# Level products of keys moved to VectorE, one copy moved earlier on ScalarE, and diagonal scores from summed keys

## The reference

```python
z = h @ w_in                     # q, v, zf, zb, og, u, gz
k = (1.0 - lb) * sigmoid(-z)     # keys kf (forward), kb (backward)
f = exp(log_f)                   # decays, one per channel and token
# per direction, 8 heads of 128 channels:
scores = einsum('t d, t s d, s d -> t s', q, decay, k)   # decay: product of f between s and t
o = scores @ v + (q * exp(b)) @ s_start
o = o_forward + flip(o_backward)
o = o * rsqrt(mean(o * o) + EPS) * hgrn_norm_g * silu(og)
# then the convolution branch, gates, w_out, the router and
# out = sum over the top 8 of 64 experts of silu(h @ gate) * (h @ up) @ down
```

## Time and profile before

| | |
|---|---|
| median of 3 runs | 904.22 us (902.78 to 906.89) |
| the profiled execution | 905.2 us, of which the profiled span is 903.4 us |
| TensorE busy | 831.0 us, 92% of the span |
| VectorE busy | 387.5 us, 43% |
| ScalarE busy | 215.3 us, 24% |
| POOL busy | 91.6 us, 10% |
| moved by DMA | 284.70 MB, mean 315 GB/s |

### The profile page before, as it was taken

One profiled execution on the slowest core, in us unless ns is written; L12 is line 12 of the kernel. 1 busy time (PEld: TensorE's weight loads), 2 busy tenths in 40 slices (PEclk: granted clock), 3 DMA queues, 4 the chain that ended last, 5 costly groups with the idle time before them and its releaser, 6 DMA issues.

```text
span 903.4 us, 12822 instructions
## 1 busy us (share of the span) xinstructions
PE 831.0 (92%) x5242; PEld 561.4 (62%) x5242; DVE 387.5 (43%) x760; ACT 215.3 (24%) x335; POOL 91.6 (10%) x63
## 2 busy tenths in 40 slices
PE   4699999999899999998999999779999999899973
PEld 2388989569899988995535544435554755345221
DVE  1225898369799846736232322111212111112104
ACT  3124443133354334403111111101111101011001
POOL 1000536205243310000000000000000000000000
PEclk9899999999899999979999999979999999999987
DMA  8979878135234538973999999999999999999993
GB/s 316 386 253 338 309 268 317 39 103 174 67 123 135 193 110 268 410 301 119 377 378 418 418 416 415 418 416 417 416 417 410 418 414 417 417 417 417 418 400 142
DMA packets 81173, 284.70 MB, mean 315 GB/s; under 512 B 5208, under 2 KB 11736, under 8 KB 64728
## 3 DMA queue, kind: packets, MB, share of 16 engines
q1 hardware_dynamic: 80760, 283.11, 80.5%
q10 hardware_dynamic: 352, 0.74, 0.3%
HBM read 280.67 MB, written 3.16 MB: 314 GB/s over the span
## 4 chain that ended last, share of the span: by engine, by line
PE 71%; SPq 12%; DMA 10%; DVE 4%; issue 2%; ACT 0%; POOL 0%; DVEq 0%; POOLq 0%
PE bank L1979 14%; SPq L591 10%; PE bank L2028 8%; PE bank L1588 5%; DMA chunk<-in_w_expert_down 5%; PE bank L1590 5%; PE bank L1596 5%; PE bank L1870 4%; PE bank L1893 4%; PE bank L1576 3%; PE bank L1650 3%; PE bank L1630 3%; DMA ring<-in_w_ada 2%; DMA chunk<-in_w_expert_gate_up 2%; PE bank L1544 2%
## 5 line engine op out<-in xcount | busy, mean ns | idle before, releaser
L1979 PE MATMUL bank<-chunk,xg 128*64 128x512 f32 (+2 forms) x1024 | 200.3, 616 | 21.2 <-DMA chunk<-in_w_expert_gate_up 19.9
L1979 PEld LDWEIGHTS bank<-chunk,xg 128*64 128x64 f32 (+2 forms) x1024 | 62.7, 130 | 153.5 <-issue 137.5
L2028 PE MATMUL bank<-chunk,act_t 128*64 128x512 f32 (+2 forms) x512 | 102.3, 623 | 5.1 <-DMA chunk<-in_w_expert_down 5.0
L1407 DVE SCALAR_TENSOR_TENSOR act_r<-bank,w_slot,sil 128x256 f32<-128x256 f32 x26 | 12.5, 482 | 181.5 <-ACT sil L933 181.5
L645 POOL TENSOR_TENSOR small<-small 128x4 f32<-128x4 f32 (+2 forms) x9 | 10.2, 1138 | 599.2 <-DVE small L1484 501.1
L1419 DVE TENSOR_TENSOR y_lo<-bank,y_hi 128x512 fp32r<-128x512 f32 x52 | 36.0, 691 | 76.4 <-ACT y_hi L946 76.4
L2028 PEld LDWEIGHTS bank<-chunk,act_t 128*64 128x64 f32 (+2 forms) x512 | 31.3, 130 | 54.7 <-issue 53.8
L933 ACT ACTIVATE sil<-bank 128x256 f32<-128x256 f32 x26 | 10.0, 385 | 203.4 <-PE bank L1979 203.4
L1032 DVE TENSOR_TENSOR ring_lo<-ring,ring_hi 128x1024 fp32r<-128x1024 f32 x40 | 47.9, 1220 | 20.4 <-ACT ring_hi L742 20.4
L946 ACT ACTIVATE y_hi<-bank 128x512 fp32r<-128x512 f32 x52 | 31.1, 597 | 105.2 <-PE bank L2028 105.2
L1870 PE MATMUL bank<-sel_p,h_hi 128*128 128x256 f32 x208 | 52.4, 293 | 2.3 <-DVE h_lo L1299 2.3
(11 more groups left out here) (293 smaller groups left out, 1323.2 us busy)
## 6 DMA issues: line engine op xcount, KB each, us to landing
chunk<-in_w_expert_gate_up SPq DMA_DIRECT2D x128, 1024.0 KB, 20.6
chunk<-in_w_expert_down SPq DMA_DIRECT2D x64, 1024.0 KB, 22.6
ring<-in_w_in SPq DMA_DIRECT2D x16, 2048.0 KB, 10.6
ring<-in_w_ada SPq DMA_DIRECT2D x12, 2048.0 KB, 13.4
ring<-in_w_proj_hgrn SPq DMA_DIRECT2D x2, 2048.0 KB, 8.1
ring<-in_w_out SPq DMA_DIRECT2D x2, 2048.0 KB, 13.5
ring<-in_w_proj_conv SPq DMA_DIRECT2D x1, 2048.0 KB, 7.8
chunk<-in_w_shared_gate_up SPq DMA_DIRECT2D x2, 1024.0 KB, 23.4
```

The costliest lines, as they stand in the source:

```text
L1979: ins = mm(bank[2 + b][row:row + width, :], xg[:, k, c:c + width], w[:, k % 4, :], start=(k == 0), stop=(k == KD - 1))
L2028: ins = mm(out[row:row + width, :], act_t[:, c, row:row + width], w[:, c, h * 512:(h + 1) * 512], start=(c == 0), stop=(c == 1))
```

## The change

Four things are changed.

- POOL no longer multiplies keys. VectorE does it, ahead of the query products of the same level, after it has read the level's scores. It waits for `mix_done` before it overwrites the keys; what it signals is `k_done` as before.
- ScalarE's copy of blended keys for level 2 stands ahead of the sigmoid of og1's first half, and no longer behind it. The copies of the other levels keep their place. The copy of level 0 waits for the scores of level −1, since `k_mix` and the new `k_sum` share their memory.
- POOL adds forward and backward keys into `k_sum`, the first four heads after their keys, the last four after theirs. TensorE makes the scores of level −1 with one matmul per head and sequence instead of two.
- POOL's inverse root for the convolution's normalisation (L645) was between its products of levels 2 and 3. It now stands alone.

```diff
--- before.py
+++ after.py
@@ -183,6 +183,7 @@
         rows_dw = at("rows_dw", 198, [P, P])
         s_new = at("s_new", 197, [P, 16, P])
         k_mix = at("k_mix", 197, [P, 16 * P])
+        k_sum = at("k_sum", 197, [P, 16 * P])
         w_r = at("w_r", 181, [P, KD, NE])
         c_pad = at("c_pad", 205, [P, KD, 32])
         mod_cols = at("mod_cols", 205, [NS * KD, 2 * P])
@@ -665,22 +666,11 @@
                                                     ALU.mult, ALU.add).then_inc(fk_done, 1)
                             nc.gpsimd.tensor_scalar(qk[:, 2 + d, c], qk[:, 2 + d, c], oml[:, i:i + 1], None,
                                                     ALU.mult).then_inc(fk_done, 1)
-            pool.wait_ge(fk_done, 32)
-
-            for level in range(LEVELS):
-                m = 1 << level
-                if level == 3:
-                    pool.wait_ge(cms_done, 1)
-                    rsqrt(rms_c, ssq_c, 2).then_inc(crms_done, 1)
-                pool.wait_ge(sc_ready, 4 * (level + 2))
-                pool.wait_ge(mix_done, level + 1)
-                if level:
-                    pool.wait_ge(tot_done, level)
-                kf, kb = halves(qk[:, 2, :], level), halves(qk[:, 3, :], level)
-                tf, tb = halves(fg[:, 0, :], level), halves(fg[:, 1, :], level)
-                nb = 16 * P // (2 * m)
-                nc.gpsimd.tensor_tensor(kf[:, :, 0, :], kf[:, :, 0, :], tf[:, :, 1, 0:1].broadcast_to([P, nb, m]), ALU.mult).then_inc(k_done, 1)
-                nc.gpsimd.tensor_tensor(kb[:, :, 1, :], kb[:, :, 1, :], tb[:, :, 0, 0:1].broadcast_to([P, nb, m]), ALU.mult).then_inc(k_done, 1)
+                pool.wait_ge(fk_done, 16 + 17 * half)
+                c = slice(half * 4 * T, (half * 4 + 4) * T)
+                nc.gpsimd.tensor_tensor(k_sum[:, c], qk[:, 2, c], qk[:, 3, c], ALU.add).then_inc(fk_done, 1)
+            pool.wait_ge(cms_done, 1)
+            rsqrt(rms_c, ssq_c, 2).then_inc(crms_done, 1)
             for g in range(4):
                 pool.wait_ge(oms_done, g + 1)
                 rsqrt(rms_o[:, 4 * g:4 * g + 4], ssq_o[:, 4 * g:4 * g + 4], 4).then_inc(orms_done, 1)
@@ -782,7 +772,7 @@
                     act.wait_ge(k_done, 2 * level)
                     act.wait_ge(sc_ready, 4 * (level + 1))
                 else:
-                    act.wait_ge(fk_done, 32)
+                    act.wait_ge(sc_ready, 4)
                 dst = halves(k_mix[:, :], level)
                 nc.scalar.activation(dst[:, :, 0, :], halves(qk[:, 2, :], level)[:, :, 0, :], ACT.Copy)
                 nc.scalar.activation(dst[:, :, 1, :], halves(qk[:, 3, :], level)[:, :, 1, :], ACT.Copy).then_inc(mix_done, 1)
@@ -804,14 +794,16 @@
             for half in range(2):
                 for j in range(2):
                     n = half * 2 + j
+                    if n == 2:
+                        mix_keys(2)
                     filled(act, f"og{half}", j)
                     if n < 2:
                         act.wait_ge(mod_ready, 12)
                     else:
                         evacuated(act, f"og{(n - 2) // 2}", n % 2)
                     nc.scalar.activation(tmp[:, n % 2, :], fill_bank(f"og{half}", j)[:, :], ACT.Sigmoid).then_inc(og_sig, 1)
-                    if j == 0:
-                        mix_keys(1 + half)
+                    if n == 0:
+                        mix_keys(1)
                     split_hi(apart + 1 + half, (3,) if j else (0, 1, 2))
             for name, dst in (("ga", ga), ("gb", gb)):
                 for half in range(2):
@@ -1080,7 +1072,7 @@
 
             score_tiles(-1)
 
-            dve.wait_ge(fk_done, 32)
+            dve.wait_ge(fk_done, 34)
             for d in (1, 0):
                 V.tensor_tensor(qk[:, 1 - d, :], qk[:, 1, :], fg[:, d, :], ALU.mult).then_inc(q_done, 1)
             dve.wait_ge(q_done, 2)
@@ -1122,8 +1114,12 @@
                 nb = 16 * P // (2 * m)
                 qb, qf = halves(qk[:, 0, :], level), halves(qk[:, 1, :], level)
                 tf, tb = halves(fg[:, 0, :], level), halves(fg[:, 1, :], level)
+                kf, kb = halves(qk[:, 2, :], level), halves(qk[:, 3, :], level)
                 if level:
                     dve.wait_ge(tot_done, level)
+                dve.wait_ge(mix_done, level + 1)
+                V.tensor_tensor(kf[:, :, 0, :], kf[:, :, 0, :], tf[:, :, 1, 0:1].broadcast_to([P, nb, m]), ALU.mult).then_inc(k_done, 1)
+                V.tensor_tensor(kb[:, :, 1, :], kb[:, :, 1, :], tb[:, :, 0, 0:1].broadcast_to([P, nb, m]), ALU.mult).then_inc(k_done, 1)
                 V.tensor_tensor(qf[:, :, 1, :], qf[:, :, 1, :], tf[:, :, 0, 0:1].broadcast_to([P, nb, m]), ALU.mult).then_inc(q_done, 1)
                 V.tensor_tensor(qb[:, :, 0, :], qb[:, :, 0, :], tb[:, :, 1, 0:1].broadcast_to([P, nb, m]), ALU.mult).then_inc(q_done, 1)
 
@@ -1643,9 +1639,7 @@
                     for i in range(4):
                         out, at_ = bank[4 + n % 2][:, i * P:(i + 1) * P], 4 * g + i
                         if level < 0:
-                            q = qk[:, 1, at_ * P:(at_ + 1) * P]
-                            mm(out, qk[:, 2, at_ * P:(at_ + 1) * P], q, start=True, stop=False)
-                            ins = mm(out, qk[:, 3, at_ * P:(at_ + 1) * P], q, start=False, stop=True)
+                            ins = mm(out, k_sum[:, at_ * P:(at_ + 1) * P], qk[:, 1, at_ * P:(at_ + 1) * P], start=True, stop=True)
                         else:
                             ins = mm(out, k_mix[:, at_ * P:(at_ + 1) * P], query_mix(level, at_), start=True, stop=True)
                     ins.then_inc(sc_ready, 1)
@@ -1670,7 +1664,7 @@
                 quarter(name, 1)
                 quarter(name, 2)
                 if level == -1:
-                    pe.wait_ge(fk_done, 32)
+                    pe.wait_ge(fk_done, 34)
                     evacuated(pe, "q1", 1)
                 else:
                     pe.wait_ge(q_done, 2 * (level + 1))
```

## The result

The changed kernel takes **894.18 us** (median of 4, 890.60 to 898.08) against 904.55 us of the kernel before on the same chip: ratio 0.9884, 95% interval 0.985 to 0.9918. Measured again later it was 892.11 us (median of 6), ratio 0.9875 (0.984 to 0.9911). The forecast was 892 us, within 888.5 to 898.

A forecast was written before the change was run, and what follows sets the result against it. TensorE was taken to bound the edited level stage, memory the expert stage. Savings 3.5 + 0.65 + 4.11 + 2.9 + 0.68 = 11.8 us took 905.2 to 893.4, less 1.0 over the median: 892 us, range 888.5 to 898.

The forecast's parts named there:

- level −1, half the matmuls: Level −1 scores: summed keys leave one of each two matmul pieces, so TensorE saves 16 x 0.22 = 3.5 us.
- level 1 copy: ScalarE's level 1 copy of blended keys no longer waits for POOL, so TensorE's 0.65 us standstill goes.
- level 2 stall: Before the level 2 scores: the copy moved ahead of the og1 sigmoid removes TensorE's 4.11 us standstill.
- clock behind it: Between the level 2 scores' halves: without the slow clock, 7.56 us becomes 4.66, saving 2.9 us.
- level 3: Between the level 3 halves: shorter VectorE products end TensorE's wait, 5.34 to 4.66 us, saving 0.68 us.
- The product's own price: A VectorE key or query product alone costs 1.08 to 1.13 us; its longer rows include waiting turns with POOL.
- A: Rival: strided products run at half rate from level 1 on, giving about 900 us; chance 0.07.
- C: Rival: VectorE becomes the bound of the level loop at 2.8 us a product, about 919 us; chance 0.06.
- Rival D: Moved level 2 copy still comes late; only scores and short gaps gain, 4.8 us, giving 899 us; chance 0.05.
- At least 4.5 us of v0 matmuls hide it: Before level −1: POOL's second key sum ends at least 4.5 us before TensorE asks, so it costs 0.
- Arrival at the end: After the level stage: no backlog crosses over, the last stage moves as a block, first expert load near 332.
- Rival B: Some load or the expert stage does not move though TensorE comes earlier: 898 to 904 us; chance 0.06.

The follow-up runs named there:

- vec_only: The kernel before with only the four products of each level put on VectorE: 900.99 us, ratio 0.9971.
- move_only: The kernel before with only the level 2 copy of blended keys moved ahead of the og1 sigmoid: 900.26 us, ratio 0.9961.
- pool_reads: The changed kernel with two idle POOL products per level at levels 0 to 3, reading and writing a tile nothing else uses: 899.46 us, ratio 0.995.
- pool_writes: The changed kernel with two POOL fills per level at levels 0 to 3, which write an otherwise unused tile and read nothing: 893.75 us, ratio 0.9884.
- before_again: The kernel before, unchanged, run again for a second profile: 903.27 us, ratio 1.0005.
- sum_move: The changed kernel without the products on VectorE, so summed keys and moved level 2 copy only: 897.12 us, ratio 0.9937.
- sum_only: The kernel before with only the summed keys, one score matmul per head and sequence at level −1: 900.07 us, ratio 0.9962.
- sum_vec: The changed kernel with the level 2 copy back behind the og1 sigmoid: 896.07 us, ratio 0.9915.
- before_third: The kernel before, unchanged, a third profile: 904.95 us, one execution.
- after: The changed kernel's first profile, against the kernel before: its slowest execution, 898.08 us; median 894.18 us, ratio 0.9884.
- after_again: The changed kernel once more, for a second profile and more times, against the kernel before: 892.11 us, ratio 0.9875.

## Why the prediction held, and where it did not

| step | foreseen | measured |
|---|---|---|
| level −1, half the matmuls | 3.5 | 3.6: from the first v0 matmul to v1's fourth quarter, 36.6 to 33.0 us |
| level 1 copy | 0.65 | 0.65, no wait left |
| level 1 between halves | none | 0.3: 5.15 to 4.87 us; comes with the products on VectorE (4.87 in vec_only, 5.16 in move_only) |
| level 2 stall | 4.11 | 4.11, no wait left |
| clock behind it | 2.9 | 2.9, 1.5 and 2.4: halves apart 7.57, 6.11, 7.04 us in three profiles of before, 4.66 after |
| level 3 | 0.68 | 0.68: 5.34 to 4.66 us |
| levels in all | 11.8 | 12.5 against the first profile of before, 11.1 and 12.0 against the others |

**Right, and shown.** The product's own price was read from the two ends 1.08 us apart rather than from its rows, and four products step by 1.13 us. pool_reads and pool_writes show that the reading, and not just the number, was right; this also settles rivals A and C: the products (L1121 to L1124, levels 0 to 6, the strided ones of the first levels among them) last 1.20 to 1.23 us at every level, and the product's old length was the turn it waited for. Rival D, the change doing only half, fell with the copy that ended 5.2 us ahead, the margin foreseen, because VectorE entered level 1 as worked out. (The prediction's 223.6 and two copies of 1.05 make 225.7, not 225.8; nothing hangs on it.)

**Right in size, wrong in security.** "At least 4.5 us of v0 matmuls hide it" was said of the summed keys. In the changed kernel POOL's second sum begins at 168.64 and ends at 170.99, and TensorE's level −1 matmuls begin at 171.47: 0.5 us. The sum itself cost less than foreseen (2.35 us against 2.9 to 3.88), but the POOL pieces ahead of it moved. One gate piece (L665) lasted 10.29 us, beside VectorE's 32 convolution taps:

```profile
150.18 12.74 DVE L1052 SCALAR_TENSOR_TENSOR conv<-upad,dw,conv 128x256 f32<-128x256 f32 x32
```

POOL came through at 163.35, 0.4 us after the last tap (162.92). In the first profile of before the taps took 14.35 us, and POOL's pieces came through between them, so that its last ended at 164.31. In before_again it was like in the changed kernel, with POOL's last at 169.8. So the change is not needed for it: the kernel before has it in one of three profiles, and which form comes varies between executions of one program. (Kernels with summed keys have it in seven of eight profiles, the others in three of six; whether that is more than chance is open.) The step that failed is the one that took POOL's end from one profile as fixed. The term 0 held by half a microsecond in both profiles of the changed kernel and in five others with summed keys (0.43 to 0.48 us); in the eighth, sum_move, POOL came through between the taps and 5.9 us were to spare. The second sum took 2.34 or 2.35 us in all eight. With the 3.13 us of sum_move's first sum, 0.3 us of stall would have shown.

**The clock term.** 2.9 us was read from one execution; in two others it is 1.5 and 2.4, and in sum_only, which keeps the stall, 2.4. The forecast had the largest of the four, and that the levels still came out at 11.1 to 12.5 us is in part luck: the 0.3 us between the halves of level 1, which the forecast had at nothing, fills some of the gap. The forecast's own argument was right that the clock falls only behind the long stall: 1.58 and 1.59 us of standing still, in sum_vec and vec_only, left it at 1.00 (4.74 us between halves), and so did 1.85 us in pool_reads; 4.10 us did not.

**Arrival at the end.** That no backlog crosses over held: the expert loads came 13.6 us earlier, and the experts' part, with a DMA share of 1.00 from 430 to 885 us, is as long as in before_third within 0.3 us. The profiled execution of after still gave back 3.1 us in the router and 1.7 each in the experts' part and the tail; with 1.0 less in the start the span is 7.1 us shorter. after_again has −11.5 against before_again: −11.1 in the levels, +1.4 in the experts' part, and −1.7 in start and tail, where two profiles of before differ by 1.4 us without a change. Rival B in its size, a stage that does not move (898 to 904 us), is refuted by the medians, 10.4 and 11.5 us below those of before. A smaller form, 1 to 1.5 us given back in the experts' part more often than before loses them, is not excluded.

## What to carry to other kernels

Where two engines run instructions of the same kind side by side and both look slow, compare the ends of pairs before adding durations: a constant distance between them is the work's own price, and moving both onto one engine can make that engine shorter. Then test the reading with idle work on the other engine, once reading and once only writing. A cover read from one profile is only as firm as the engine's queue ahead of it: look for a piece whose length depends on who got the turn, and count its long form. When two parts remove the same stall, measure each beside the others and not alone.

## What the runs showed of the hardware that had not been expected

- VectorE can keep POOL out for a whole row of instructions: 10.29 us for a POOL gate piece beside 32 taps, ending 0.4 us behind the last tap, where the next such piece takes 0.55 us. It was so in 10 of the 14 profiles of all kernels (10.18 to 10.32 us, taps 12.74 to 12.89 us); in the other four the pieces alternate, and the taps take 14.35 us in three and 16.30 in sum_move. That the engines take turns there too is read from the ends; no run varied it.
- The TensorE clock makes single executions of one program differ by microseconds at fixed places: 11.6 or 14.8 us for one chain of narrow matmuls, 3.65 or 5.35 us for 16 matmuls of 128x512, 1.5 to 2.9 us behind a 4.1 us stall. With these places, the two profiles of the changed kernel differ by 7.2 us of span. A comparison of two profiles has to be made part by part before a difference is given to the edit.
- Standing still for up to 1.85 us cost TensorE's clock nothing here (1.50 to 1.59 us in four profiles, 1.85 in pool_reads); 4.1 us did in each of the four profiles that have it.
